# Shift and scale in four parts of 256 features, the first six W_in blocks summed over two K chunks at a time, upper chunks of x transposed behind the lower

## The chip, the cores and the metric

The kernel runs on one core of a Trainium2 chip. Its time is the device time of one execution in microseconds (us). Before the change three runs took 943.0, 944.63 and 945.49 us, median 944.63. The profiled execution took 942.63 us; the span from its first to its last instruction is 940.9 us.

The engines are named as in the profile: PE is TensorE (matrix products and transposes; PEld its weight loads), DVE VectorE, ACT ScalarE, POOL GpSimd, SP SyncE, which issues nearly all loads of weights. Each runs its own instructions in order and waits on semaphores that others raise.

## The reference

One encoder layer is applied to two requests of 256 tokens with 1024 features. Cut to what the change touches:

```
mod = (silu(c) @ w_mod + b_mod).reshape(B, 6, 1, D)        # c: (B, 1024), w_mod: (1024, 6144)
shift1, scale1, gate1 = mod[:, 0], mod[:, 1], mod[:, 2]    # and shift2, scale2, gate2
h = LN(x) * (1 + scale1) + shift1                          # (256, 1024) for each request
z = h @ w_in + b_in                                        # w_in: (1024, 5120): u, v, p, gates
a = gelu(u) * (W_s @ LN(gelu(v)) + b_s)                    # v is the segment computed first
...                                                        # pooling branch, merge, W_out, LN
out = mixture of experts: top group of 4, top 2 of its 8 experts, 32 experts of 3 x 2 MB
```

All is float32. Large products split each operand in a high part (rounded to the type fp32r) and the remainder as a low part, and sum three products: high x high, low x high, high x low.

## The kernel before

Tokens of both requests lie side by side (512 columns), features on the partitions in 8 chunks of 128 (`KC = 8`). The stages in order are: load x, its mean and variance (DVE), normalise (DVE), transpose on PE to chunks of features, copy out of PSUM (ACT) into `n_t`; shift and scale of the features; then 56 blocks of 128 output features (`NBLK`), 5.5 us of PE each in the steady state; then the output projection, routing and 32 experts.

The change lies in the first 60 us. Shift and scale come from `w_mod[:, 0:2048]` (8 MB). Before the change this is done in two parts of 512 features each, because h of chunk 0 needs the sum over all 1024 rows of `w_mod` but only its own columns:

- `first_mod_unit(part, q)` multiplies two row chunks of `w_mod` by silu(c) into the PSUM bank `MOD`. The four products of one round (shift and scale, two row chunks) go to four groups of 32 columns of the array. Four units make a part. DVE adds the bias (`first_mod_rows`), PE transposes the row into columns in bank `COL` (`first_mod_columns`), DVE sums and adds 1 (`first_scales`).
- With the scales of a part, ACT writes the high half of h, `h_hi` (`h_high`), DVE and POOL the full h in `h32`, and DVE the low half `h_lo` (`h_low`).
- The first six blocks of W_in (`FIRST = 6`) are summed in the same two parts of 4 chunks, in six PSUM banks kept open. ACT writes the high part of a piece of W_in (`part_split_hi`), DVE the low part (`first_split_lo`, `split_lo`). Blocks 0 and 1 go as a pair, chunk by chunk as h arrives (`part_pair`), the others in turn (`part_block`). After the second part's pair, ACT evaluates gelu on finished blocks and PE transposes them back (`transposes`).
- `keep_clock` is a product whose result nobody reads.

SP issues the loads in one queue and in this order: x, part 0 of `w_mod` (8 loads of 512 KB), part 0 of W_in, part 1 of both, then `load_mod(8)` and on: the 16 loads of 1 MB with the other 4096 columns of `w_mod`, into two buffers in turn (`modraw`), used by `mod_unit_at` between blocks, and among them `load_unit(2)`, the next 2 MB of W_in. `load_mod(m)` waits until `m - 1` units have been multiplied (`pe_mod`), since its buffer must be free. A load of an expert or of W_in later in the kernel is released by the work on PE in the same way. POOL issues 2.3 MB of loads for later stages (`ws_raw`, `wp_raw`, `bs_bc` and small ones) when all of `h_lo` is written (`pool.wait_ge(dve_hlo, KC)`); PE needs `ws_raw` after block 5, just ahead of unit 2 of `mod_unit_at`.

Of the kernel before, what the change touches and what calls it, by code (L numbers as in the profile page):

```python
# [36 lines left out]
PART = KC // 2  # L37
H_DIRECT = (0, 1, 4, 5)
H_VECTOR = (3, 0, 7, 4)
H_POOL = (2, 1, 6, 5)  # L40


def hybrid_encoder(nc, x_prompt, x_sample, c_prompt, c_sample, w_mod, b_mod, w_in, b_in, w_spatial,
# [12 lines left out]
    with ctx:  # L56
# [5 lines left out]
        def sem(name):  # L62
# [20 lines left out]
        modraw0 = [at(f"modraw0_{i}", [128, 2, 2, 512], f32, o)  # L83
                   for i, o in enumerate([2 * SLOT + 8 * K * j for j in range(4)] + [32 * K, 40 * K] + [SLOT + 32 * K, SLOT + 40 * K])]
# [42 lines left out]
        modrow_first = at("modrow_first", [128, 2, 512], f32, S0 + 9728 + 4096)  # L127
# [259 lines left out]
        def first_mod_source(part, kc):  # L387
            return w_mod[0, 128 * kc:128 * kc + 128, 0:2048].rearrange("p (v f n) -> p v f n", v=2, f=2)[:, :, part, :]

        def halves_of_chunks(tiles, turn):  # L390

            first = PART * (turn // 2 % 2)
            return tiles[turn % 2][:, first:first + PART, :]

# [44 lines left out]
        def _(sp):  # L439
            def load_unit(u):  # L440
                if u >= 2:
                    sp.wait_ge(dve_wlo, FIRST + 4 * (u - 1))
# [8 lines left out]
            for part in range(2):  # L451
                for kc in range(KC):
                    m = 4 * part + kc // 2
                    landed = s_m0[4 + kc // 4 if part else kc // 2]
                    sp.dma_start(modraw0[m][:, kc % 2, :, :], first_mod_source(part, kc)).then_inc(landed, 16)
                chunks = slice(PART * part, PART * part + PART)
                if part == 0:
# [3 lines left out]
                    sp.dma_start(raw[:, 1, chunks, :], unit_source(1)[:, chunks, :]).then_inc(s_wpre[2], 16)  # L461
                else:
                    for u in range(2):
                        sp.dma_start(raw[:, u, chunks, :], unit_source(u)[:, chunks, :]).then_inc(s_w[u], 16)
# [93 lines left out]
        def _(pool):  # L558
# [4 lines left out]
            for v in range(2):  # L563
                for r in range(REQ):
                    pool.dma_start(modrow_first[64 * v + r:64 * v + r + 1, :, :],
                                   b_mod[0:1, 1024 * v:1024 * v + 1024].rearrange("a (f n) -> a f n", f=2)).then_inc(s_bmod, 16)
# [4 lines left out]
            for kc in H_POOL:  # L571
# [142 lines left out]
        def _(pe):  # L714
# [15 lines left out]
            def first_mod_unit(part, q):  # L730
# [4 lines left out]
                for k in range(2):  # L735
                    for v in range(2):
                        j = 2 * v + k
                        x = mm(MOD[32 * j:32 * j + 32, :], silu_c[:, 2 * q + k, :], modraw0[4 * part + q][:, k, v, :], start=(q == 0), stop=(q == 3))
                x.then_inc(pe_mod, 1)

            def first_mod_columns(part):
                pe.wait_ge(dve_row0, part + 1)
                for k in range(4):
# [3 lines left out]
            for _ in range(3):  # L747
                keep_clock(512)
            pe.wait_ge(act_pro, 1)

            def n_columns(i):
                pe.wait_ge(dve_n, i + 1)
                if i >= 2:
                    pe.wait_ge(act_nt, 2 * (i - 1))
                for kc in range(KC):
                    bank = B[2 * (i % 2) + kc // 4]
                    x = pe.transpose(bank[:, 128 * (kc % 4):128 * (kc % 4) + 128], xin[:, i, 128 * kc:128 * kc + 128], ident)
                x.then_inc(pe_xt, 1)

            first_mod_unit(0, 0)  # L760
            n_columns(0)
            n_columns(1)
            first_mod_unit(0, 1)
            n_columns(2)
            n_columns(3)
            first_mod_unit(0, 2)
            first_mod_unit(0, 3)
            keep_clock(256)
            pe.wait_ge(act_nt, 2 * TILES)
            pe.wait_ge(dve_pro, 1)  # L770
            first_mod_columns(0)
            keep_clock(512)
# [1771 lines left out]
```

## Time and profile before

| | |
|---|---|
| median of three runs | 944.63 us |
| the profiled execution | 942.63 us, span 940.9 us |
| PE busy | 897.1 us, 95% of the span |
| DVE, ACT, POOL busy | 381.0, 243.1, 118.1 us |
| moved by DMA | 295.3 MB, mean 314 GB/s |
| first product of h with W_in | 27.16 us from the start |
| end of the pair of part 1 | 54.34 us from the start |

The profile's times are microseconds from the span's start. A timeline row is: start, duration, engine, line, operation, output<-input, shapes, number of instructions merged, and in brackets how long the engine was idle before it and who released it. One float32 product or unit product shows as two records of MATMUL (a product of 128x512 in the form fp32r as one). A DMA row gives the number of DMAs, KB each and the median time from issue to landing.

### The profile page before, as it was taken

Reading aid. Unit: us, or ns where it says so; the run is one execution under the profiler, and the core shown is the slowest. Engines: PE = TensorE matmul, PEld = TensorE weight load, DVE = VectorE, ACT = ScalarE, POOL = GpSimd, SP = SyncE. Lnnn points to the kernel's source line nnn. Section 1 sums busy time; section 2 is a strip of 40 time slices with the busy share of each in tenths; the row PEclk is TensorE's granted clock in tenths of the full one; section 3 lists DMA queues with packets and bytes.
Section 4 is the critical chain, followed back from the end, with each engine's and each line's share of the span. In section 5 each row is a group of like instructions: output and inputs, shape, how many; then the busy total and the mean of one; then the engine's idle time right before and its main releaser. Section 6 shows DMA issues by size and latency. Waiting matters only on the chain. (4 is left out here: it accounts for less than half of the span.)

```text
span 940.9 us, 12139 instructions
## 1 busy us (share of the span) xinstructions
PE 897.1 (95%) x4420; PEld 547.3 (58%) x4420; DVE 381.0 (40%) x657; ACT 243.1 (26%) x360; POOL 118.1 (13%) x149
## 2 busy tenths in 40 slices
PE   5999999999999999999999999998998999999894
PEld 2677767888888888787544444444444344444331
DVE  5543434565344236798622322222122132321346
ACT  3342335331333225446410111011011101110113
POOL 3130556000001000000000000000000100000041
PEclk9999999999999999999999999999999999999997
DMA  9975676274665623908999999999999999999993
GB/s 341 363 246 191 224 269 224 90 267 179 222 225 153 183 90 101 300 1 367 399 384 419 427 426 426 426 427 427 429 426 425 424 387 428 429 427 427 422 412 122
DMA packets 51291, 295.32 MB, mean 314 GB/s; under 512 B 5438, under 2 KB 6558, under 8 KB 35986
## 3 DMA queue, kind: packets, MB, share of 16 engines
q1 hardware_dynamic: 40784, 263.47, 69.9%
q0 software_dynamic: 9952, 29.80, 9.4%
q10 hardware_dynamic: 482, 1.13, 0.3%
q8 instruction: 39, 0.64, 0.3%
q14 instruction: 34, 0.28, 0.1%
HBM read 275.81 MB, written 22.83 MB: 317 GB/s over the span
## 5 line engine op out<-in xcount | busy, mean ns | idle before, releaser
L716 PE MATMUL banks<-down_w,hid_t 128*64 128x512 f32 x512 | 119.7, 610 | 11.9 <-issue 10.9
L716 PE MATMUL banks<-h_hi,w_hi 128*128 128x512 f32 x320 | 125.0, 391 | 0.5 <-ACT h_hi L1398 0.5
L716 PE MATMUL banks<-h_lo,w_hi 128*128 128x512 f32 x320 | 125.2, 398 | 0.0
L716 PE MATMUL banks<-h_hi,w_lo 128*128 128x512 f32 x320 | 124.8, 390 | 0.0
L716 PE MATMUL banks<-up_w,x_by_expert 128*64 128x512 f32 x256 | 112.6, 593 | 0.0
L716 PE MATMUL banks<-gate_w,x_by_expert 128*64 128x512 f32 x256 | 112.5, 592 | 0.0
L716 PE MATMUL banks<-up_w,x_by_pair 128*64 128x512 f32 x240 | 105.4, 592 | 0.0
L716 PE MATMUL banks<-gate_w,x_by_pair 128*64 128x512 f32 x240 | 105.4, 592 | 0.0
L1615 ACT ACTIVATE sg_hid<-banks 64x512 f32<-64x512 f32 x33 | 19.5, 592 | 313.8 <-PE banks L716 313.8
L2177 DVE TENSOR_TENSOR sg_hid<-banks,sg_hid 64x512 f32<-64x512 f32 x32 | 22.2, 694 | 177.9 <-ACT sg_hid L1615 177.9
L685 POOL DMA_INDIRECT round_y<-yout,store_row x30 | 31.0, 1034 | 461.5 <-DVE yout L2300 448.7
L1806 DVE TENSOR_TENSOR w_lo<-raw,w_hi 128x1024 fp32r<-128x1024 f32 x50 | 61.4, 1228 | 67.0 <-ACT w_hi L1353 66.9
L716 PEld LDWEIGHTS banks<-down_w,hid_t 128*64 128x64 f32 x512 | 36.3, 140 | 72.2 <-issue 65.2
L716 PEld LDWEIGHTS banks<-gate_w,x_by_expert 128*64 128x64 f32 x256 | 34.9, 137 | 70.8 <-issue 70.7
L1353 ACT ACTIVATE w_hi<-raw 128x1024 fp32r<-128x1024 f32 (+1 forms) x62 | 59.8, 970 | 61.2 <-PE banks L716 54.3
L716 PEld LDWEIGHTS banks<-h_lo,w_hi 128*128 128x128 f32 x320 | 60.1, 188 | 25.1 <-issue 8.4
L716 PEld LDWEIGHTS banks<-gate_w,x_by_pair 128*64 128x64 f32 x240 | 32.9, 137 | 66.5 <-issue 66.5
L716 PE MATMUL banks<-sel_group,h_hi 128*128 128x256 f32 x256 | 69.7, 306 | 0.0
L2300 DVE TENSOR_TENSOR yout<-banks,yout 128x512 f32<-128x512 f32 x32 | 22.1, 691 | 112.9 <-PE banks L716 112.8
L716 PEld LDWEIGHTS banks<-h_hi,w_hi 128*128 128x128 f32 x320 | 60.2, 188 | 12.7 <-ACT h_hi L1398 1.1
L716 PEld LDWEIGHTS banks<-h_hi,w_lo 128*128 128x128 f32 x320 | 60.1, 188 | 12.7
L716 PE MATMUL banks<-sel_group,h_lo 128*128 128x256 f32 x256 | 63.6, 282 | 1.4 <-issue 1.4
(331 smaller groups left out, 1314.7 us busy)
## 6 DMA issues: line engine op xcount, KB each, us to landing
down_w<-in_w_exp_down SPq DMA_DIRECT2D x29, 2048.0 KB, 20.5
gate_w<-in_w_exp_gate SPq DMA_DIRECT2D x28, 2048.0 KB, 18.5
up_w<-in_w_exp_up SPq DMA_DIRECT2D x28, 2048.0 KB, 22.9
modraw<-in_w_mod SPq DMA_DIRECT2D x16, 1024.0 KB, 4.9
raw<-in_w_in SPq DMA_DIRECT2D x8, 2048.0 KB, 9.7
round_y<-zrow POOLq DMA_DIRECT2D x6, 2048.0 KB, 7.6
modraw<-in_w_mod SPq DMA_DIRECT2D x16, 512.0 KB, 11.4
down_w<-in_w_exp_down SPq DMA_DIRECT2D x6, 1024.0 KB, 14.8
```

The costliest lines, as they stand in the source:

```text
L685: pool.indirect_dma_start(round_halves, bass.IndirectOffsetOnAxis(store_row[:, e:e + 1], 0), yout[s][:, :], None, bounds_check=2 * LAST_RO ...
L716: return pe.matmul(out, lhsT, rhs, start=start, stop=stop, skip_group_check=True)
L1353: return act.activation(out, in_, ACT.Copy, scale=scale)
L1615: act.activation(sgb[0:CAP, :], bank[0:CAP, :], ACT.Silu).then_inc(sm["silu"], 1)
L1806: dve.tensor_tensor(w_lo[par][:, :, :], raw[:, u % 2, :, 128 * (b % 4):128 * (b % 4) + 128], w_hi[par][:, :, :].bitcast(f32), ALU.subtract ...
L2177: dve.tensor_tensor(sg_hid[CAP:128, :], B[0][CAP:128, :], sg_hid[0:CAP, :], ALU.mult).then_inc(m_sem["hid"], 1)
L2300: dve.tensor_tensor(yout[s][:, :], B[1][:, :], yout[s][:, :], ALU.mult).then_inc(m_sem["yo"], 1)
```

## The change

The constant `NPART = 4` takes the place of two parts: a part is now 2 chunks of 128 features (`PART = 2`), with 256 columns each of shift and scale (`WIDE = 256`). It does the following.

- The 8 MB of `w_mod` come in 32 loads of 256 KB, and W_in in pieces of 2 chunks. PE waits for 4 loads, then for 8, in part 0, and for all 8 of a part after that. The units of a part (products 256 wide) stand together behind block 2 of the part before.
- The transposes of x are cut in lower chunks (0 to 3) and upper chunks (4 to 7). The lower ones come first; the upper ones of tiles 1 to 3 follow the column transposes of part 0. On ACT, `n_copied` of the upper chunks stands behind `h_high(0)` and block 2's split.
- All eight chunks of `h_hi` are written by ACT directly from `n_t`; even chunks of `h32` come from DVE, odd ones from POOL.
- Of three `keep_clock(512)` ahead of the first unit one is left, and the two behind the column transposes are gone.
- `load_mod(8)` waits for 8 units instead of 7 (`max(KC, m - 1)`); `pe_mod` now counts two units at a time, two per part, so that it reaches 8 in part 3's units.
- The first six blocks are multiplied in four parts, in banks kept open over all four.

```
-PART = KC // 2
-H_DIRECT = (0, 1, 4, 5)
-H_VECTOR = (3, 0, 7, 4)
-H_POOL = (2, 1, 6, 5)
+NPART = 4
+PART = KC // NPART
+WIDE = 128 * PART
+BEFORE = FIRST * (NPART - 1)
...
             def load_mod(m):
-                sp.wait_ge(pe_mod, m - 1)
+                sp.wait_ge(pe_mod, max(KC, m - 1))
...
-            for part in range(2):
+            for part in range(NPART):
                 for kc in range(KC):
-                    m = 4 * part + kc // 2
-                    landed = s_m0[4 + kc // 4 if part else kc // 2]
-                    sp.dma_start(modraw0[m][:, kc % 2, :, :], first_mod_source(part, kc)).then_inc(landed, 16)
+                    landed = s_m0[part + 1 if part else kc // 4]
+                    sp.dma_start(modraw0[part][kc // 2][:, kc % 2, :, :], first_mod_source(part, kc)).then_inc(landed, 16)
...
-            for kc in H_POOL:
+            for kc in range(1, KC, 2):
                 pool.wait_ge(dve_col, 2 * (kc // PART) + 2)
...
+            def first_mod_units(part, first, last):
                 if part == 0:
-                    pe.wait_ge(s_m0[q], 32)
+                    pe.wait_ge(s_m0[first // 2], 64)
                 else:
-                    pe.wait_ge(s_m0[4 + q // 2], 64)
...
+                    pe.wait_ge(s_m0[part + 1], 128)
+                for q in range(first, last):
+                    for k in range(2):
+                        for v in range(2):
+                            j = 2 * v + k
+                            x = mm(MOD[32 * j:32 * j + 32, 0:WIDE], silu_c[:, 2 * q + k, :], modraw0[part][q][:, k, v, :], start=(q == 0), stop=(q == 3))
+                    if q % 2 == 1:
+                        x.then_inc(pe_mod, 1)
...
-            for _ in range(3):
-                keep_clock(512)
+            keep_clock(512)
             pe.wait_ge(act_pro, 1)
...
-            part_pair(0)
-            first_mod_unit(1, 0)
-            part_block(0, 2)
-            first_mod_unit(1, 1)
-            part_block(0, 3)
-            first_mod_unit(1, 2)
-            first_mod_unit(1, 3)
-            part_block(0, 4)
-            pe.wait_ge(dve_col, 1)
-            first_mod_columns(1)
-            part_block(0, 5)
-            part_pair(1)
+            for part in range(NPART - 1):
+                part_pair(part)
+                part_block(part, 2)
+                first_mod_units(part + 1, 0, 4)
+                part_block(part, 3)
+                first_mod_columns(part + 1)
+                part_block(part, 4)
+                part_block(part, 5)
+            part_pair(NPART - 1)
...
             for i in range(TILES):
-                act.wait_ge(pe_xt, i + 1)
-                for hb in range(2):
-                    copy(n_t[:, 4 * hb:4 * hb + 4, 128 * i:128 * i + 128],
-                         B[2 * (i % 2) + hb][:, :].rearrange("p (k n) -> p k n", k=4)).then_inc(act_nt, 1)
...
+                n_copied(i, 0)
             part_split_hi(0, 0)
             part_split_hi(0, 1)
+            act.wait_ge(act_nt, TILES)
             h_high(0)
-            for b in range(2, FIRST):
-                part_split_hi(0, b)
-            part_split_hi(1, 0)
-            part_split_hi(1, 1)
-            h_high(1)
+            part_split_hi(0, 2)
+            n_copied(0, 1)
+            n_copied(1, 1)
+            part_split_hi(0, 3)
+            n_copied(2, 1)
+            n_copied(3, 1)
+            part_split_hi(0, 4)
+            part_split_hi(0, 5)
+            act.wait_ge(act_nt, 2 * TILES)
+            for part in range(1, NPART):
+                part_split_hi(part, 0)
+                part_split_hi(part, 1)
+                h_high(part)
+                if part < NPART - 1:
+                    for b in range(2, FIRST):
+                        part_split_hi(part, b)
...
+            for part in range(NPART):
+                first_mod_rows(part)
+                part_split_lo(part, 0)
+                if part:
+                    part_split_lo(part, 1)
+                first_scales(part)
+                dve.wait_ge(dve_col, 2 * part + 2)
+                if part == 0:
+                    part_split_lo(part, 1)
+                elif part == 2:
+                    dve.wait_ge(act_nt, 2 * TILES)
+                modulated(PART * part)
+                for kc in range(PART * part, PART * part + PART):
+                    h_low(kc)
+                if part < NPART - 1:
+                    for b in range(2, FIRST):
+                        part_split_lo(part, b)
```

PE, before, from the first product on the constants to the first product of h with W_in (`cst` are constants, `modraw` pieces of `w_mod`, `xin` normalised rows of x, `modrow_first` shift and scale as rows):

```order
L716 MATMUL banks<-cst 128x512 x3
L716 MATMUL banks<-modraw_0_68,silu_c 32x512 x4
L757 MATMUL banks<-cst,xin 128x128 x16
L716 MATMUL banks<-modraw_1_69,silu_c 32x512 x4
L757 MATMUL banks<-cst,xin 128x128 x16
L716 MATMUL banks<-modraw_2_70,silu_c 32x512 x4
L716 MATMUL banks<-modraw_3_71,silu_c 32x512 x4
L716 MATMUL banks<-cst 128x256
L744 MATMUL banks<-cst,modrow_first 128x128 x4
L716 MATMUL banks<-cst 128x512
L716 MATMUL banks<-cst 128x256
L716 MATMUL banks<-h_hi,w_hi_80 128x512
```

PE, after, the same place:

```order
L719 MATMUL banks<-cst 128x512
L719 MATMUL banks<-modraw_0_0_68,silu_c 32x256 x4
L719 MATMUL banks<-modraw_0_1_69,silu_c 32x256 x4
L719 MATMUL banks<-cst 128x256
L766 MATMUL banks<-cst,xin 128x128 x12
L719 MATMUL banks<-modraw_0_2_70,silu_c 32x256 x4
L719 MATMUL banks<-modraw_0_3_71,silu_c 32x256 x4
L766 MATMUL banks<-cst,xin 128x128 x8
L751 MATMUL banks<-cst,modrow_first 128x128 x2
L766 MATMUL banks<-cst,xin 128x128 x12
L719 MATMUL banks<-h_hi,w_hi_88 128x512
```

Twelve of the 32 transposes of x have moved behind the column transposes, and the units are half as wide.

ACT, before, from the copies of the transposed x to the pieces of W_in that follow `h_hi` (`n_t` is x normalised and transposed, `h` the full h):

```order
L1353 ACTIVATE n_t<-banks 128x4x128 x8
L1353 ACTIVATE w_hi_80<-raw 128x512
L1353 ACTIVATE w_hi_81<-raw 128x512
L1398 ACTIVATE h_hi<-n_t,mod_t,scale1p 128x256 x4
L1353 ACTIVATE h_hi<-h_115 128x512 x2
L1353 ACTIVATE w_hi_80<-raw 128x512
L1353 ACTIVATE w_hi_81<-raw 128x512
```

ACT, after, the same place:

```order
L1359 ACTIVATE n_t<-banks 128x4x128 x4
L1359 ACTIVATE w_hi_88<-raw 128x256
L1359 ACTIVATE w_hi_89<-raw 128x256
L1405 ACTIVATE h_hi<-n_t,mod_t,scale1p 128x256 x4
L1359 ACTIVATE w_hi_88<-raw 128x256
L1359 ACTIVATE n_t<-banks 128x4x128 x2
L1359 ACTIVATE w_hi_89<-raw 128x256
L1359 ACTIVATE n_t<-banks 128x4x128 x2
```

Four of the eight copies of x now stand behind `h_hi`, and the first splits are half as wide.

## Rows read from the trace of the kernel before

**Rows 1.** The page, part 1: busy time, share of the span, instructions.

```profile
PE 897.1 (95%) x4420; PEld 547.3 (58%) x4420; DVE 381.0 (40%) x657; ACT 243.1 (26%) x360; POOL 118.1 (13%) x149
```

**Rows 2.** Timeline of PE up to the first product of h with W_in.

```profile
10.37 5.49 PE L716 MATMUL banks<-cst 128*128 128x512 f32 x6
...
18.93 1.06 PE L716 MATMUL banks<-modraw,silu_c 128*32 128x512 f32 x8
19.93 1.97 PE L757 MATMUL banks<-cst,xin 128*128 128x128 f32 x16
21.82 1.92 PE L716 MATMUL banks<-modraw,silu_c 128*32 128x512 f32 x16
...
25.20 1.46 PE L716 MATMUL banks<-cst 128*128 128x512 f32 x4
27.16 0.50 PE L716 MATMUL banks<-h_hi,w_hi 128*128 128x512 f32 x1 [0.51 <-ACT h_hi L1398]
```

**Rows 3.** Timeline of DVE: normalising, first scales, one full split.

```profile
14.05 2.98 DVE L1786 TENSOR_SCALAR xin<-xin,mv,rs 128x1024 f32<-128x1024 f32 x4
...
23.89 0.69 DVE L1816 TENSOR_TENSOR modrow_first<-banks,modrow_first 128x512 f32<-128x512 f32 x1 [6.73 <-PE banks L716]
24.50 0.68 DVE L1811 TENSOR_TENSOR w_lo<-raw,w_hi 128x512 fp32r<-128x512 f32 x1
25.40 0.17 DVE L1822 COPY mod_t<-banks 128x16 f32<-128x16 f32 x1 [0.21 <-PE banks L744]
...
68.79 1.22 DVE L1806 TENSOR_TENSOR w_lo<-raw,w_hi 128x1024 fp32r<-128x1024 f32 x1 [0.54 <-ACT w_hi L1353]
```

**Rows 4.** Timeline of ACT: copies, first splits, first h_hi, one full split.

```profile
21.06 2.06 ACT L1353 ACTIVATE n_t<-banks 128x512 f32<-128x512 f32 x4 [0.83 <-PE banks L757]
22.98 1.17 ACT L1353 ACTIVATE w_hi<-raw 128x512 fp32r<-128x512 f32 x2
26.02 2.08 ACT L1398 ACTIVATE h_hi<-n_t,mod_t,scale1p 128x256 fp32r<-128x256 f32 x4 [1.86 <-DVE scale1p L1825]
...
67.71 1.05 ACT L1353 ACTIVATE w_hi<-raw 128x1024 fp32r<-128x1024 f32 x1
```

**Rows 5.** Loads issued from 1.8 to 3.0 us: KB each, us to landing.

```profile
modraw<-in_w_mod SPq DMA_DIRECT2D x2, 512.0 KB, 10.0
```

**Rows 6.** Windows: PE, PEld, DVE, ACT, POOL busy, granted clock, DMA share, GB/s.

```profile
10.00:15.00 5.00, 4.93 (x7) 2.02 (x7) 4.45 (x14) 1.69 (x3) 0.00 (x0) 1.00 1.06 382
```

**Rows 7.** Timeline of PE: part 1's pair, and what follows it.

```profile
48.73 0.39 PE L716 MATMUL banks<-h_hi,w_hi 128*128 128x512 f32 x1
...
52.36 1.98 PE L716 MATMUL banks<-h_lo,w_hi 128*128 128x512 f32 x8
54.89 0.66 PE L825 MATMUL banks<-cst,g 128*128 128x128 f32 x4 [0.55 <-ACT g L1432]
...
71.54 1.06 PE L716 MATMUL banks<-modraw,silu_c 128*32 128x512 f32 x8
...
78.64 1.06 PE L716 MATMUL banks<-modraw,silu_c 128*32 128x512 f32 x8
```

**Rows 8.** Timeline of SP's queue: load_mod(10), load_unit(2).

```profile
56.60 0.33 SPq L447 DMA_DIRECT2D modraw<-in_w_mod  x1
57.30 0.38 SPq L443 DMA_DIRECT2D raw<-in_w_in  x1
```

**Rows 9.** Loads issued at 56.6 us: load_mod(10), beside POOL's.

```profile
modraw<-in_w_mod SPq DMA_DIRECT2D x1, 1024.0 KB, 11.3
```

**Rows 10.** Loads issued at 57.3 us: load_unit(2).

```profile
raw<-in_w_in SPq DMA_DIRECT2D x1, 2048.0 KB, 16.6
```

**Rows 11.** Loads issued at 64.2 us: load_mod(11).

```profile
modraw<-in_w_mod SPq DMA_DIRECT2D x1, 1024.0 KB, 12.2
```

**Rows 12.** Loads issued from 41 to 43 us: load_mod(8) and (9).

```profile
modraw<-in_w_mod SPq DMA_DIRECT2D x2, 1024.0 KB, 5.6
```

**Rows 13.** Timeline of POOL: the first of its loads.

```profile
51.90 0.99 POOL L579 DMA_DIRECT2D ws_raw<-in_w_spatial  x1 [2.64 <-DVE h_lo L1840]
```

More of the change, by code:

```diff
@@ L741, in first_mod_columns @@
             def first_mod_columns(part):
                 pe.wait_ge(dve_row0, part + 1)
-                for k in range(4):
+                if part:
+                    pe.wait_ge(dve_col, 2 * part - 1)
+                for k in range(PART):
                     x = pe.transpose(COL[:, 128 * k:128 * k + 128], modrow_first[:, part, 128 * k:128 * k + 128], ident)
                 x.then_inc(pe_modcol, 1)
-            for _ in range(3):
-                keep_clock(512)
+            keep_clock(512)
@@ L749, in _ @@
             pe.wait_ge(act_pro, 1)
[L751 to L757, printed above, removed]
-                x.then_inc(pe_xt, 1)
-            first_mod_unit(0, 0)
-            n_columns(0)
@@ L762, in _, with n_columns @@
[L762 to L767, printed above, removed]
-            keep_clock(256)
-            pe.wait_ge(act_nt, 2 * TILES)
+            def n_columns(i, hb):
+                bank = B[i if hb == 0 else (4, 5, 0, 1)[i]]
+                if hb == 0:
+                    pe.wait_ge(dve_n, i + 1)
+                elif i >= 2:
+                    pe.wait_ge(act_nt, i - 1)
+                for k in range(4):
+                    first = 512 * hb + 128 * k
+                    x = pe.transpose(bank[:, 128 * k:128 * k + 128], xin[:, i, first:first + 128], ident)
+                x.then_inc(pe_xt, 1)
@@ L770, in _ @@
+            first_mod_units(0, 0, 2)
+            keep_clock(256)
+            n_columns(0, 0)
+            n_columns(0, 1)
+            n_columns(1, 0)
+            first_mod_units(0, 2, 4)
+            n_columns(2, 0)
+            n_columns(3, 0)
             pe.wait_ge(dve_pro, 1)
             first_mod_columns(0)
-            keep_clock(512)
-            keep_clock(256)
+            for i in range(1, TILES):
+                n_columns(i, 1)
             def block_at(b, i, mov_hi, mov_lo, freed, count):
-                pe.wait_ge(act_whi, FIRST + b + 1)
-                pe.wait_ge(dve_wlo, FIRST + b + 1)
+                pe.wait_ge(act_whi, BEFORE + b + 1)
+                pe.wait_ge(dve_wlo, BEFORE + b + 1)
@@ new lines, in n_copied, with h_high @@
+            def n_copied(i, hb):
+                act.wait_ge(pe_xt, ((1, 3, 4, 5), (2, 6, 7, 8))[hb][i])
+                copy(n_t[:, 4 * hb:4 * hb + 4, 128 * i:128 * i + 128],
+                     B[i if hb == 0 else (4, 5, 0, 1)[i]][:, :].rearrange("p (k n) -> p k n", k=4)).then_inc(act_nt, 1)
+            def h_high(part):
+                act.wait_ge(dve_col, 2 * part + 2)
+                for kc in range(PART * part, PART * part + PART):
+                    for r in range(REQ):
+                        x = act.activation(h_hi[:, kc, SEQ * r:SEQ * r + SEQ], n_t[:, kc, SEQ * r:SEQ * r + SEQ], ACT.Identity,
+                                           scale=scale1p[:, kc, r:r + 1], bias=mod_t[:, 0, kc, r:r + 1])
+                    x.then_inc(act_hhi, 1)
```

124 lines of the change are left out of this document (45 added, 79 removed).

## The prediction

> **What bounds the kernel now.** I read the page's busy times first: PE works 95% of the span [rows 1], so a microsecond counts only where PE stands still or is given more or less work. Next came PE's timeline up to the first product of h with W_in [rows 2]: that product starts at 27.16 us, released by ACT. Behind it PE has work without a break until the pair of part 1 ends at 52.36 + 1.98 = 54.34 us [rows 7]. What comes later than 27.16 only because the start is late moves up with it, unless a load is missing. So two questions decide: how much earlier the start is, and whether the loads issued between 41 and 65 us, which wait for PE, can follow.
>
> The chain to the start, from the timelines of DVE and ACT: the last unit ends at 21.82 + 1.92 = 23.74; DVE adds the bias at 23.89 and ends the first scales at 26.0 [rows 3]; ACT writes h_hi 0 at 26.02 in two instructions of 0.52 [rows 4]; PE starts at 27.16.
>
> **The start, step by step.** Rows of x are normalised from 14.05, one every 0.745 (2.98 / 4) [rows 3]; this doesn't change. The first two loads of `w_mod`, 512 KB each, issued at 1.9 and about 2.4, take 10.0 us [rows 5], so the first megabyte is there at about 12.8; the new first four loads are the same bytes. The second megabyte follows at 382 GB/s [rows 6], 1.05 MB / 382 GB/s = 2.7 us later: 15.6. Before, two further megabytes were needed.
>
> PE: the first products on constants run at half the pace: 5.49 / 3 = 1.83 us for 128x512 [rows 2], against 1.46 us for one of 512 and one of 256 at 25.20, or 0.97 for 512. That is the 1.2 GHz level against 2.4, though the granted clock already reads 1.00 there [rows 6]; I go by the pace. One such product: to 12.2. PE waits until 12.9. A unit 512 wide at full pace costs 1.92 - 1.06 = 0.86 us [rows 2]; at half width and half pace the same: two, with 0.3 at the ends, to 14.9; the product of 256 on constants to 15.8. Before, full pace was there at 17 us, after 6 us of work; I take it here from 15.8. Twelve transposes at 1.97 / 16 = 0.12 [rows 2]: 17.3. Two units of 0.43 and 0.15: 18.3. Eight transposes: 19.3. ACT then copies the last lower chunk, 0.52 [rows 4]: 19.9; splits block 0, 256 wide. A split of 512 costs 1.17 / 2 = 0.58, one of 1024 1.05 [rows 4]; 256 is not in the trace. Its bounds are 0.2 (half of 512, no fixed part) and 0.58; the line through the two rows gives 0.35 to 0.4, which I take: 20.3. DVE's low part (0.68 at 512, 1.22 at 1024 [rows 3], so 0.42): 20.75. The scales follow it in DVE's order, 25.40 to 26.02 = 0.62: 21.4. Two instructions of ACT and the hand-over, 1.14 as before: **first product at 22.6, 4.5 us earlier.** Both queues of waits matter here: behind DVE's split, which waits for ACT, stand the scales that ACT waits for.
>
> **What moves behind the start.** Before, four units ran after the first product: two alone at 1.06 - 0.06 and two together at 1.86, 3.9 us. Now twelve of half width do: 12 x 0.43 + 3 x 0.15 = 5.6. Half width might not halve the time; bounds 0.25 and 0.86 a unit, 3.5 and 10.8 in all; since the four column groups work side by side and each round is 0.43 long at 512, I stay near half. Column transposes: three times two for once four, 0.75 for 0.36 (0.66 with its tail for four [rows 7]). Gaps between groups: +0.2. Together 2.3 us. The 144 products of the six blocks are the same number in both kernels, as is their pace, (52.36 - 48.73) / 16 = 0.227 [rows 7]. The lead when block 5 ends is thus **4.5 - 2.3 = 2.2 us**.
>
> The other edits cost nothing on the path. ACT now writes all eight h_hi with 2 x 0.52 each where two of four had 0.57, about 2 us more ACT work; a part holds 36 x 0.227 + 1.9 + 0.4 + 0.5 = 10.9 us of PE work and 6.5 of ACT's. If that cover were gone, 0.5 us per part would show. The upper copies stand behind h_hi 0 and 1; block 2 needs the first at about 25.4, and it is done near 24.4. The twelve late transposes, 1.5 us, fit between 19.6 and 22.6, where PE waits anyway. The 8 loads of part 1 are wanted at 22.6 + 4.1 = 26.7 and land near 24 (another 0.8 + 2.1 MB behind 15.6 at 382 GB/s is 23.2). After that a part's 3.1 MB comes every 8.3 us, and PE takes 10.9 us for a part, so the slack grows.
>
> **What the lead meets.** The end of the pair of the last part: 22.6 + 120 x 0.227 + 5.6 + 0.75 + 1.4 (the gaps that the same stretch has now, 27.18 - 96 x 0.227 - 3.9 - 0.36 = 1.1, for 120 products) = 57.6, **3.3 us later** than 54.34, though only half a part is left after it. And that point, not block 5, releases the loads: load_mod(10) waits for the unit behind the pair (issued 56.60 now [rows 8], then about 59.7), load_unit(2) for the split of block 3 behind the pair (57.30 now [rows 8], then about 60), POOL's 2.3 MB for the last h_low (51.90 now [rows 13], then about 55.5). The loads of 8 and 9 are issued at 50.3 instead of about 42 and take 5.6 [rows 12]: in time.
>
> load_mod(10) lands 11.3 us after its issue, being moved beside POOL's loads [rows 9]: at 67.9 now, at 71.0 then. PE uses it at 71.54 now [rows 7]; with blocks 2 to 5 at 1.37 us instead of 2.74 it wants it at 57.6 + 17.2 - 5.5 = 69.3 and **waits 1.7**. Then one unit, block 6 and transposes (71.54 to 78.64, 7.1 us [rows 7]): 78.1. Unit 3 needs load_mod(11), which stands behind load_unit(2) in SP's queue: that one lands at 57.30 + 16.6 = 73.9 [rows 10] and load_mod(11) at 64.2 + 12.2 = 76.4 [rows 11], so the queue, not its issue, sets it. The queue starts 3.1 us later with the same bytes: 79.5. Bounds: 76.4 if the queue makes up everything, 80.2 if POOL's shift of 3.6 counts in full. I take 79.5, from the shift of the SP loads. Now unit 3 starts at 78.64. **Sum: 79.5 - 78.64 = +0.9 us**; behind it PE has its loads in time (load_mod(12) is issued behind unit 2 and used a whole block later than 11), and the difference stays to the end.
>
> 942.63 + 0.9 = 943.5 in terms of the profiled execution. This one lies 2.0 under the median of the runs, so I predict 944.63 + 0.9 = **945.5 us**.
>
> **The rivals.** *The lead survives.* The loads come in time since load_mod(10) and POOL's loads overlap less than now. For it: 10 and 11 have 3.6 and 2.2 us in hand now. Against: both are issued by the event that moves later. Gives -2.2: 942.4. Chance 0.20.
>
> *The start is earlier still.* If the low splits and scales follow sooner (PE at full pace from the beginning, 1.2 us less; splits at 0.2, 0.4 less), the start is near 21, the pair ends at 56, the loads cost nothing: -3.8, 940.8. Against: nothing shows full pace before 16 us. Chance 0.12.
>
> *PE stays at half pace.* The two removed products leave it idle from 12.2 to 12.9 and feed it narrow units. If full pace comes one stretch of work later, near 19, the 12 transposes cost 1.5 more and the two units 0.9: start 24.9, pair end 59.9, the queue 5.4 later, load_mod(11) at 81.8: +3.1, **947.7**, slower. It decides from about 1 us of half pace behind 15.8. For it: the busy stretch before full pace was unbroken. Chance 0.15.
>
> *Small loads.* If a load of 256 KB takes the 1.36 us of 512 KB, the eight of part 0 land where they do now, the start stays at 27.2, the pair ends at 62.2, load_mod(11) at 84.1: +5.5, 950.1. For it, nothing in the rows but that no load of this size is there; 512 KB at a time the queue gives 382 GB/s [rows 6]. Chance 0.05.
>
> On this last case the Trainium skill (DMA: Bandwidth & Descriptors, section Rules for kernel authors) says that one should have at least 1 MiB per DMA for the most bandwidth. The trace's 382 GB/s with half of that doesn't bear it out for loads that queue one behind the other, which is why the chance is small.
>
> **How the numbers follow.** Forecast 0.48; its own range 943.8 to 947. A measurement tells this kernel from no change at about 0.3%, 2.8 us. Faster by more (under 941.8): 0.10 of the second rival, 0.08 of the first, 0.02 of the forecast: 0.20. Slower by more (over 947.4): 0.09, 0.05, and 0.05 of the forecast: 0.19. The same: 0.61. The range 941.2 to 948.8 leaves out the small loads and the ends of the others.
>
> **What would show it.** First product of h with W_in at 22.6 (21.5 to 25). Units of four at 1.9 us a part. End of the last part's pair at 57.6. PE idle ahead of unit 2, released by the load, 1 to 3 us; again ahead of unit 3, up to 1.5. Unit 3's start against 78.64 is the whole effect: if it is under 77, the lead survived and the step on the queue is wrong; if the first product is later than 24, the clock or the loads' size is it. A change of span that differs from unit 3's shift would put the cause behind 80 us, where I claim none.

## The result, and the profile after

The changed kernel took 951.12 us, median of five runs (945.48 to 953.11), against 944.63 (943.0 to 945.49; by now five runs too) before: ratio 1.0063, 95% interval 1.0045 to 1.0082. Forecast were 945.5, a range of 941.2 to 948.8, and a chance of 0.19 for slower. Nine more runs in a second set gave 948.62 (945.97 to 952.21) against 944.17, ratio 1.0046 [1.0027, 1.0065]. So by the ratios the change costs 4 to 6 us where +0.9 was forecast. The profiled execution (945.48 us, span 943.8) is the fastest of its five, so its trace holds the smallest part of the loss. Below, unit n is the n-th unit of `mod_unit_at`, counted from 0, which multiplies what load_mod(8 + n) brings.

The page, part 1, answers to [rows 1]: PE has less work than before and a longer span.

```profile
span 943.8 us, 12332 instructions
PE 895.0 (95%) x4476; PEld 548.7 (58%) x4476; DVE 382.8 (41%) x677; ACT 246.6 (26%) x376; POOL 118.5 (13%) x149
```

PE's timeline up to the first product of h with W_in, after (columns as in [rows 2]):

```profile
10.46 2.07 PE L719 MATMUL banks<-cst 128*128 128x512 f32 x2
14.08 1.93 PE L719 MATMUL banks<-modraw,silu_c 128*32 128x256 f32 x16 [1.55 <-DMA modraw<-in_w_mod]
15.95 1.22 PE L719 MATMUL banks<-cst 128*128 128x256 f32 x2
16.96 2.77 PE L766 MATMUL banks<-cst,xin 128*128 128x128 f32 x12
19.66 1.40 PE L719 MATMUL banks<-modraw,silu_c 128*32 128x256 f32 x16
20.99 1.09 PE L766 MATMUL banks<-cst,xin 128*128 128x128 f32 x8
21.92 0.38 PE L751 MATMUL banks<-cst,modrow_first 128*128 128x128 f32 x2
22.14 1.47 PE L766 MATMUL banks<-cst,xin 128*128 128x128 f32 x12
25.25 0.50 PE L719 MATMUL banks<-h_hi,w_hi 128*128 128x512 f32 x1 [1.63 <-ACT h_hi L1405]
```

The first megabyte is there at 14.1, not 12.9, in a stretch that now moves 344 GB/s instead of 382 [rows 6] (its first loads of 256 KB take 8.7 us, those of 512 KB took 10.0 [rows 5]). Not only the loads are smaller: from 10 to 20 us 3775 of 3790 packets are under 2 KB, where before 459 of 2277 were. The first twelve transposes take 2.77 us, while the last twelve take 1.47: half pace lasts until about 20 us, not 15.8. The product that was forecast for 22.6 comes at 25.25.

```profile
10.00:15.00 5.00, 3.28 (x15) 1.22 (x19) 4.45 (x14) 1.69 (x3) 0.00 (x0) 1.00 1.11 344
```

ACT's and DVE's rows for the narrow splits, after, answer to [rows 3, 4]: two splits of 256 take 0.72 on ACT, one low part 0.42 on DVE, as estimated.

```profile
22.66 0.72 ACT L1359 ACTIVATE w_hi<-raw 128x256 fp32r<-128x256 f32 x2
```

```profile
23.11 0.42 DVE L1826 TENSOR_TENSOR w_lo<-raw,w_hi 128x256 fp32r<-128x256 f32 x1 [1.47 <-ACT w_hi L1359]
```

PE's timeline from the last part's units on, after; it answers to [rows 7]:

```profile
50.67 1.93 PE L719 MATMUL banks<-modraw,silu_c 128*32 128x256 f32 x32
...
58.81 1.07 PE L719 MATMUL banks<-h_lo,w_hi 128*128 128x512 f32 x4
...
71.42 1.09 PE L861 MATMUL banks<-cst,ws_raw 128*128 128x128 f32 x8 [0.65 <-DMA bs_bc<-in_b_spatial]
72.95 1.07 PE L719 MATMUL banks<-modraw,silu_c 128*32 128x512 f32 x8 [0.44 <-DMA modraw<-in_w_mod]
...
83.23 1.07 PE L719 MATMUL banks<-modraw,silu_c 128*32 128x512 f32 x8 [3.10 <-DMA modraw<-in_w_mod]
```

Before, PE waits at none of these places, and unit 3 starts at 78.64; now it waits 0.65 + 0.44 + 3.10 us and starts unit 3 at 83.23, 4.6 later. The first of the three waits is for POOL's `bs_bc`, which the prediction didn't name. This shift goes on to the experts' first load, which PE's work releases. SP's queue there, before and then after:

```profile
380.43 0.34 SPq L478 DMA_DIRECT2D gate_w<-in_w_exp_gate  x1
```

```profile
385.02 0.34 SPq L481 DMA_DIRECT2D gate_w<-in_w_exp_gate  x1
```

The queues, after, answer to [rows 8 to 13]. POOL's first load comes at 58.22, 6.3 us later than before:

```profile
58.22 1.00 POOL L582 DMA_DIRECT2D ws_raw<-in_w_spatial  x1 [1.84 <-DVE h_lo L1852]
```

load_mod(8) and (9) are issued at 52.7 and take 5.9 us, load_mod(10), issued at 62.1, takes 10.8, and load_unit(2) and load_mod(11), issued at 62.52 and 66.99, the following (DMA rows of one issue each). 66.99 + 16.2 = 83.2 is the start of unit 3.

```profile
raw<-in_w_in SPq DMA_DIRECT2D x1, 2048.0 KB, 18.2
```

```profile
modraw<-in_w_mod SPq DMA_DIRECT2D x1, 1024.0 KB, 16.2
```

The span itself grew by 2.9 us only (940.9 to 943.8), 1.7 less than unit 3's shift. The prediction would read such a difference as a cause behind 80 us. But the stretch from the experts' first load to the end takes 558.8 to 563.6 us in the fourteen traces of this document (560.5 before), and the longest belongs to **small_before**, which has the code of the kernel before there. What moves it was not looked into; a single trace's total doesn't measure this change, so below, traces are compared at the experts' first load, and totals by the ratios.

### The profile page after: what moved, and what is told of

It is laid out like the page before. It is cut to its first block and busy times, and to the rows that moved or that the text cites. A ratio compares the mean times of both kernels' runs of the same rounds, so it can differ in the third digit from the quotient of the medians.

```text
span 943.8 us, 12332 instructions
## 1 busy us (share of the span) xinstructions
PE 895.0 (95%) x4476; PEld 548.7 (58%) x4476; DVE 382.8 (41%) x677; ACT 246.6 (26%) x376; POOL 118.5 (13%) x149
## 5 line engine op out<-in xcount | busy, mean ns | idle before, releaser
L2186 DVE TENSOR_TENSOR sg_hid<-banks,sg_hid 64x512 f32<-64x512 f32 x32 | 22.2, 695 | 184.3 <-ACT sg_hid L1630 182.9
L719 PEld LDWEIGHTS banks<-gate_w,x_by_pair 128*64 128x64 f32 x240 | 32.9, 137 | 67.3 <-issue 67.3
## 6 DMA issues: line engine op xcount, KB each, us to landing
down_w<-in_w_exp_down SPq DMA_DIRECT2D x6, 1024.0 KB, 10.8
```

The lines of the kernel that those rows point to most:

```text
L719: return pe.matmul(out, lhsT, rhs, start=start, stop=stop, skip_group_check=True)
L2186: dve.tensor_tensor(sg_hid[CAP:128, :], B[0][CAP:128, :], sg_hid[0:CAP, :], ALU.mult).then_inc(m_sem["hid"], 1)
```

## The experiments

Twelve kernels ran in three groups, each group with runs of the kernel before on the same chip (medians 944.17, 944.3 and 943.04). "Landing" is the landing of load_mod(11), counted from POOL's first load; where PE waits for it, it is the start of unit 3, and elsewhere the issue plus the time to landing. "Waits" are those of PE for loads from block 5 to unit 3. All times are us of one profiled execution, except the ratio.

| kernel | first product | POOL's first load | landing | waits | unit 3 | experts' first load | ratio to before, interval |
|---|---|---|---|---|---|---|---|
| before | 27.16 | 51.90 | 24.5 | 0 | 78.64 | 380.43 | 1 |
| changed | 25.25 | 58.22 | 25.0 | 4.2 | 83.23 | 385.02 | 1.0063 [1.0045, 1.0082] |
| again | 23.35 | 56.27 | 26.2 | 5.3 | 82.45 | 385.63 | 1.0046 [1.0027, 1.0065] |
| clock | 22.13 | 55.07 | 25.9 | 5.1 | 80.96 | 384.32 | 1.0035 [1.0020, 1.0050] |
| later | 24.63 | 57.54 | 26.4 | 0 | 84.90 (a block later) | 380.45 | 0.9981 [0.9966, 0.9996] |
| both | 22.00 | 54.97 | 26.2 | 0 | 82.36 (a block later) | 377.90 | 0.9976 [0.9961, 0.9991] |
| early | 23.64 | 56.58 | 26.1 | 5.3 | 82.71 | 387.37 | 1.0048 [1.0032, 1.0064] |
| all | 22.90 | 55.87 | 25.7 | 0 | 83.27 (a block later) | 378.88 | 0.9967 [0.9955, 0.9979] |
| pool | 24.51 | 57.48 | 22.6 | 1.7 | 80.07 | 381.86 | 1.0007 [0.9991, 1.0024] |
| fill | 23.73 | 56.69 | 25.7 | 2.1 | 85.46 | 388.21 | 1.0068 [1.0042, 1.0094] |
| small_before | 26.68 | 51.56 | 21.5 | 0 | 78.32 | 380.11 | 0.9998 [0.9987, 1.0009] |
| best | 23.30 | 56.22 | 22.6 | 0 | 83.61 (a block later) | 379.19 | 0.9974 [0.9956, 0.9992] |
| pool_clock | 23.46 | 56.46 | 22.2 | 1.4 | 78.64 | 380.46 | 0.9967 [0.9951, 0.9982] |
| fill2 | 24.71 | 57.66 | 26.0 | 2.6 | 84.22 | 386.00 | 1.0033 [1.0020, 1.0046] |

**again**, the changed kernel as it is.

> The changed kernel as it is, timed again beside the other three of this call, with a second trace. Why: its profiled execution took 945.48 us, but its median was 951.1, and the mean granted clock of its five runs went from 0.992 (945.5 us) down to 0.982 (952.6 us). Theory A (the loads): the loss up to 90 us is the same in every run, +4 to +5 us at unit 3 of mod_unit_at, and what is over it comes later, from the clock. Theory B (the early clock): in the slow runs full pace comes later still in the first 30 us, or falls again behind the 3.1 us for which PE waits ahead of unit 3. A expects unit 3 near 83 us in this trace too, B expects it at 85 or later if this trace is of a slow run. Median expected 948 to 952.

The start was nearly on forecast this time (first product 23.35, last pair's end 56.85 + 1.07 = 57.9, unit 2 at 71.3), and yet load_mod(11) landed at 82.45, three us behind its forecast. The start accounts for 0.75 of them; the rest is the queue itself. PE's rows, then windows (columns as in [rows 6]):

```profile
82.45 1.94 PE L719 MATMUL banks<-modraw,silu_c 128*32 128x512 f32 x8 [3.99 <-DMA modraw<-in_w_mod]
84.31 0.80 PE L719 MATMUL banks<-h_lo,w_hi 128*128 128x512 f32 x1
```

```profile
68.00:70.00 2.00, 1.09 (x8) 0.76 (x7) 1.74 (x2) 1.81 (x3) 0.00 (x0) 1.00 1.03 243
70.00:72.00 2.00, 1.57 (x16) 0.74 (x14) 1.31 (x2) 0.05 (x1) 0.00 (x0) 1.00 1.06 197
...
80.00:82.00 2.00, 0.00 (x0) 0.00 (x0) 0.96 (x1) 1.01 (x1) 0.00 (x0) 1.00 0.60 254
82.00:84.00 2.00, 1.55 (x8) 0.20 (x8) 0.27 (x1) 0.00 (x0) 0.00 (x0) 0.52 0.31 131
84.00:86.00 2.00, 2.00 (x9) 1.42 (x6) 0.00 (x0) 0.00 (x0) 0.00 (x0) 0.62 0.40 61
```

Two things were not in the prediction: from 68 to 72 us the queues are full (share 1.03 and 1.06) but move only 243 and 197 GB/s, and behind PE's idle time the granted clock falls to 0.52, the lower level. Unit 3 at +3.8 becomes the experts' load at +5.2. So both theories have a part: unit 3 is near 83 us as in A, and what is over it follows the wait, as in B, without a later start.

**clock**, one more product ahead of the first unit.

```
-            keep_clock(512)
+            for _ in range(2):
+                keep_clock(512)
```

> One more product on constants (128x512) ahead of the first units, where PE stood idle from 12.5 to 14.1 us. If that gap is what kept PE at half pace until about 20 us, full pace comes near 16 us, the first product of h with W_in moves from 25.3 to 23.0-23.8, unit 3 from 83.2 to about 81.5, and the kernel gains about 1.5 us on the changed one. If the gap is not it (the narrow products are), the start stays at 25 and nothing changes.

Full pace came with the first units (16 records in 1.07 us), and the first product at 22.13, against the 22.6 forecast for the change itself. But PE still waited 1.03 + 0.74 + 3.29 us, and the clock fell behind that. A start 1.2 us earlier than in **again** brought 1.3 at the experts' load; the ratio is 0.0011 lower, with intervals that overlap.

**later**: unit 2 and the transposes of ws_raw behind block 6, unit 3 behind block 7, unit 4 with unit 5.

```
-                if n == 5:
+                if n == 6:
...
-                if n in (1, 3, 5, 6, 7):
-                    mod_unit_at({1: 0, 3: 1, 5: 2}.get(n, n - 3))
+                if n in (1, 3, 6, 7):
+                    mod_unit_at({1: 0, 3: 1, 6: 2, 7: 3}[n])
...
+                if n == 0:
+                    mod_unit_at(4)
```

> Units 2 and 3 of mod_unit_at and the transposes of ws_raw one block later each (unit 2 behind block 6, unit 3 behind block 7, unit 4 beside unit 5 behind block 8); the same work on PE. Theory A (PE waits for loads that the end of the pair releases): the three waits, 0.65 + 0.44 + 3.1 = 4.2 us, go, and the end of block 6 and all behind it moves up by about 4 us; unit 5 at its place within 0.5 us of the kernel before; time 4 us under the changed kernel. Rival (PE would have lost it anyway, at the next load): the waits come back at units 3 to 5 and the gain is under 1 us.

No load is waited for, and the whole loss is gone, though the start was at half pace until about 20 us in this trace. The loss is these waits and what follows from them. load_mod(11) still lands 26.4 us behind POOL's first load, at 83.9; unit 3 now wants it at 84.90. PE's rows of units 2 and 3, then SP's of the experts' first load (380.43 before):

```profile
77.80 1.06 PE L719 MATMUL banks<-modraw,silu_c 128*32 128x512 f32 x8
...
84.90 1.06 PE L719 MATMUL banks<-modraw,silu_c 128*32 128x512 f32 x8
```

```profile
380.45 0.34 SPq L481 DMA_DIRECT2D gate_w<-in_w_exp_gate  x1
```

**both**: the last two edits together.

> Both edits, the product on constants and the later units. If each works by itself and they add, first product near 23.4, no waits, and the experts' first load is issued at 380.4 + 0.4 - 1.7 = about 379 us (380.43 before, 385.02 in the changed kernel): 1 us faster than the kernel before, within what can be told. If only the loads count, as later.

In the traces the gains add up: the start is 2.6 us earlier than in **later** and the experts' load as much, 2.5 before that of the kernel before. In the ratio 0.9976 beside 0.9981 doesn't show it, with intervals that overlap. No load is waited for; 0.77 us without a releaser stand ahead of block 6, as in **later**.

**early**: load_mod(8) and (9) issued at 38.4 us instead of 52.7, into buffers that are free by then.

```
-            [32 * K + 4 * K * j for j in range(4)], [SLOT + 32 * K + 4 * K * j for j in range(4)]))]
+            [32 * K + 4 * K * j for j in range(4)], [16 * K + 4 * K * j for j in range(4)]))]
...
-                sp.wait_ge(pe_mod, max(KC, m - 1))
+                if m >= 10:
+                    sp.wait_ge(pe_mod, m - 1)
```

> The changed kernel, with load_mod(8) and load_mod(9) (2 MB) issued right behind the first W_in pieces instead of at 52.7 us: the third part's first buffers lie in space that is free until ws_raw is written. Queue theory: in the changed kernel these 2 MB are on the queues when POOL's loads and load_mod(10) are issued, and they push the landing of load_mod(11) back; 2 MB at some 400 GB/s are 5 us, of which about 2 overlap. Without them load_mod(11) lands 1.3 to 2.4 us sooner, PE's wait ahead of unit 3 falls from 3.1 to between 1 and 2 us, the experts' first load is issued 1.3 to 2.4 us earlier (383.0 to 384.3), and the median falls by 1.5 to 2, to about 0.9970 of the changed kernel's ratio, so 1.0025 against before. Rival, the load stream from POOL's issue to load_mod(11) sets the landing by itself: no change, ratio 1.0046.

The rival holds: nothing was moved from 52 to 58 us, and load_mod(11) still landed 26.1 us behind POOL's first load. The 2 MB of load_mod(8) and (9) were not what pushed it back. The clock fell behind the wait for longer than in the runs so far (windows, granted clock third from the end):

```profile
82.00:84.00 2.00, 1.29 (x8) 0.20 (x8) 0.55 (x1) 0.00 (x0) 0.00 (x0) 0.51 0.35 147
84.00:86.00 2.00, 2.00 (x7) 1.16 (x4) 0.00 (x0) 0.00 (x0) 0.00 (x0) 0.50 0.29 53
86.00:88.00 2.00, 2.00 (x6) 1.58 (x5) 0.00 (x0) 0.00 (x0) 0.00 (x0) 0.50 0.84 315
```

Unit 3 starts 4.1 us later than before, the experts' load 6.9: 2.9 are added behind the fall.

**all**: both and early.

> The kernel with two products of 512 columns to hold the clock at the start and with units 2, 3 and 4 one block later (it measured 0.9976 against before), and with load_mod(8) and load_mod(9) issued right behind the first W_in pieces. Queue theory: PE no longer waits for a load there, so an earlier landing is worth nothing: ratio 0.9976 within 0.001, the experts' first load at 377.9. Rival, the loads still cost there in a way that the waits don't name (the 0.77 us without a releaser at block 6): 0.5 to 1 us faster.

PE waits for no load in either kernel, and the experts' load came 1.0 us later than in **both**, with the start 0.9 later. The ratio, 0.9967 beside 0.9976 with intervals that overlap, fits the theory and the rival alike.

**pool**: four small loads behind POOL's windows instead of ahead of them.

```
-            pool.dma_start(wr[:, :, 0:NGRP], w_router_group[0, :, :].rearrange("(p k) n -> p k n", p=128)).then_inc(s_wr, 16)
-            pool.dma_start(wr[:, :, NGRP:], w_router_expert[0, :, :].rearrange("(p k) n -> p k n", p=128)).then_inc(s_wr, 16)
-            pool.dma_start(br_bc[:, 0:NGRP], b_router_group[0, :].partition_broadcast(128)).then_inc(s_wr, 16)
-            pool.dma_start(br_bc[:, NGRP:], b_router_expert[0, :].partition_broadcast(128)).then_inc(s_wr, 16)
...
             pool.wait_ge(dve_d, 8)
+            (the same four)
             pool.dma_start(sgu_bc[:, 0, :], sgu_g[0, :].partition_broadcast(128)).then_inc(s_sgu, 16)
```

> The changed kernel, with POOL's four small router loads (the router's weights and biases) issued behind its pooling windows instead of ahead of them. Theory one, the queue is long because of these loads of many small pieces: bs_bc and load_mod(11) land 1 to 2 us sooner, the experts' first load comes as much earlier, the median falls by 1 to 2. Theory two, the queue is long because of its bytes, of which these loads are few: load_mod(11) within 0.5 us of where it was behind POOL's issue (24.5 to 26.4 us), ratio 1.0046 within 0.0015.

Theory two fell, and theory one forecast too little. These loads are 0.16 MB, and load_mod(11) lands 22.6 us behind POOL's first load instead of 25.0 to 26.4 in the nine traces that have them there. The windows show where; the same stretch as that shown for **again**, without the slow two:

```profile
68.00:70.00 2.00, 2.00 (x12) 1.49 (x10) 1.22 (x2) 1.81 (x3) 0.00 (x0) 1.00 0.97 391
70.00:72.00 2.00, 1.12 (x9) 0.86 (x8) 2.00 (x3) 1.26 (x2) 0.00 (x0) 1.00 1.03 389
```

The queue that POOL's loads go through tells the same, from 57 to 90 us, in the changed kernel and then in this one (packets, MB, share of 16 engines' time):

```profile
q0 software_dynamic: 736, 2.26, 27.4%
```

```profile
q0 software_dynamic: 592, 2.10, 21.9%
```

0.16 MB less frees (27.4 - 21.9)% x 33 us = 1.8 us of all 16 DMA engines, where at the 391 GB/s of the window the bytes are worth 0.4. The rest of the 2.4 us or more by which the landing moves is not accounted for. PE waits 1.7 us instead of 4.2 to 5.3, and by the two ratios the kernel is 3.7 us faster than in **again**.

**fill**: five products on constants ahead of unit 3's wait.

```
+                if n == 6:
+                    pe.wait_ge(dve_col, 8)
+                    for _ in range(5):
+                        mm(COL[:, :], ident, cst[:, 0:512])
```

> The changed kernel, with five products of 512 columns on constants ahead of unit 3's wait for its load. They add no path, since PE waits there for 3 to 4 us. Theory, a wait of PE of 4 us there makes the granted clock fall behind it (unit 3 at 1.94 instead of 1.07 us a group): with the wait cut by some 1.1 us the clock stays at 1.00 behind it, unit 3's eight groups take 1.07, and against a run with the fall the experts' first load is issued up to 0.6 us earlier; in the median 0 to 0.5 us, which three rounds can hardly tell. Rival, the fall has another source: the groups of unit 3 are at 1.9 again in the profile, at a clock of 0.5 to 0.6 from 82 to 86 us.

The pricing was wrong: it took 1.1 us for the five products, and they took 4.46, from 81.07 on. load_mod(11) landed at 82.4, so without them PE would have waited some 1.3 us, and unit 3 started 3.1 us behind the landing. (A further wait of 1.15 us for a load, at 148 us, is in this trace too.) The clock stayed at 1.00 behind them, which tells nothing, since no wait was left. It had fallen earlier in this trace, to 0.64 and 0.51 from 72 to 76 us, behind waits of 0.88 and 1.22 us for bs_bc and load_mod(10).

**small_before**: the kernel before, with the edit of **pool**.

> The kernel before the change, with POOL's four small router loads behind its pooling windows. In its trace the load rate is 253 to 300 GB/s from 64 to 68 us, and PE waits for none of these loads. Theory, the small loads lengthen the queue by 2 to 3 us in any kernel but cost only one that has no slack there: ratio 1.000 within 0.0012, PE without a wait ahead of units 2 and 3 (at 71.5 and 78.6), and 380 GB/s or more in the two-microsecond windows between 64 and 68. Rival, they cost time of their own (in POOL or DVE, or a wait that the rows don't name): faster by 0.1% or more.

The landing comes 3.0 us sooner (24.5 to 21.5) and the time is the same. The windows of 64 to 68 us, before and then with the edit, repeat what **pool** showed, at an earlier time: the small loads lengthen the queue here too, and PE waits for nothing behind them.

```profile
64.00:66.00 2.00, 2.00 (x12) 1.61 (x9) 0.67 (x1) 0.00 (x0) 0.00 (x0) 1.00 1.02 253
66.00:68.00 2.00, 2.00 (x12) 1.69 (x11) 0.44 (x1) 0.88 (x2) 0.00 (x0) 1.00 0.96 300
```

```profile
64.00:66.00 2.00, 2.00 (x10) 1.62 (x10) 0.35 (x1) 0.00 (x0) 0.00 (x0) 1.00 1.02 398
66.00:68.00 2.00, 2.00 (x13) 1.65 (x12) 0.69 (x1) 1.20 (x2) 0.00 (x0) 1.00 1.05 391
```

**best**: all, with the edit of **pool**.

> Two products to hold the clock at the start, units 2, 3 and 4 one block later, load_mod(8) and load_mod(9) early (together 0.9967 against before), and the four small router loads behind the pooling windows. PE waits for no load there any more, so by the queue theory the last edit is worth nothing: ratio 0.9967 within 0.0012, the experts' first load at 378 to 379 us. Rival, the router loads cost elsewhere: 0.5 to 1 us faster.

No further gain: 0.9974, the experts' load at 379.19, 0.3 us behind that of **all** and 0.2 outside the forecast, with a start 0.4 later.

**pool_clock**: clock, with the edit of **pool**.

> The changed kernel with two products of 512 columns at the start instead of one, and with the router loads behind the windows. The sum from the parts: first product near 22.1, end of the last pair near 56.7, POOL's first load at 55.1, load_mod(11) 22.6 us later (as in the run with the router loads moved) at 77.7, unit 3 at 78.0 to 78.7 after waits of 0.5 to 2 us in all, the experts' first load at 379.5 to 380.5, which is 0 to 1 us before the kernel before: ratio 0.9985 to 1.0000. Rival, what the clock gives is lost again in the queue, as in the run with the two products alone, where 1.3 us of start gave 0.9 to 1.3: ratio 1.0005 or more.

Unit 3 starts at 78.64, to the hundredth where it does before (that it is the hundredth is chance), and the experts' load at 380.46. In the ratio it is better than that and than forecast, 0.9967; its profiled run is the slowest of its seven, so the trace's start (23.46, full pace later than in **clock**) may not be typical. Four versions, both, all, best and pool_clock, lie at 0.9967 to 0.9976 with intervals that overlap: all are faster than before by 2.3 to 3.1 us, and the runs rank them neither against each other nor against **later**.

**fill2**: fill with two products instead of five.

> The changed kernel with two products of 512 columns on constants ahead of unit 3's wait; by the run with five (4.46 us) they take 1.8 us, of a wait of 3 to 4. Theory, waits of 3 to 4 us make the clock fall behind them in some runs and not in others, and that is the spread: unit 3 at 1.06 in the profile, no clock under 0.9 from 82 to 90 us, the median 0.5 to 1.5 us below the changed kernel's and its runs closer together, ratio 1.0030 to 1.0040. Rival, the fall does not follow from the wait, or the spread is from the experts: ratio 1.0046 or more, spread as before.

The two took 1.88 us and ended 0.6 us behind the landing of load_mod(11); unit 3 took 1.06, and no window from 82 to 90 us is under 1.00. The clock fell in another place instead, behind a wait of 2.58 us for bs_bc, which landed 15.1 us behind POOL's first load (13.2 to 13.9 in **changed**, **again**, **clock**, **early** and **fill**):

```profile
74.00:76.00 2.00, 2.00 (x9) 0.50 (x2) 0.00 (x0) 0.00 (x0) 0.00 (x0) 0.53 0.92 313
76.00:78.00 2.00, 2.00 (x7) 1.59 (x6) 0.00 (x0) 0.00 (x0) 0.00 (x0) 0.62 1.06 422
```

The ratio is 0.0013 below that of **again**, with intervals that overlap, and the experts' load, at 386.00, is not earlier than in the two traces of the changed kernel. So a gain is not shown.

## Why the prediction was wrong

**Right.** The first product of h comes earlier. What moves behind the start: the units of a part take 1.93 us (forecast 1.9), and from the first product to the end of the last pair there are 34.6 us in both traces of the changed kernel (59.88 - 25.25, 57.92 - 23.35; forecast 57.6 - 22.6 = 35.0). The lead is eaten because the release of the loads stands behind the last part. POOL's loads start 32.9 to 33.0 us behind the first product (forecast 32.9). PE waits ahead of unit 2 (1.1 and 1.3 us, forecast 1.7) and of unit 3, and where the clock doesn't fall behind it, the shift of unit 3 is what arrives at the experts (4.59 and 4.59 in the first trace, 1.43 and 1.43 in **pool**). That **pool** measures 1.0007, +0.7 us, close to the forecast +0.9, is luck: its start was 1.9 us later than forecast and its queue 1.4 shorter.

**The step that failed: "the queue starts 3.1 us later with the same bytes: 79.5".** The prediction took the queue as a fixed length and moved it by the shift of SP's loads, 0.5 below POOL's. By its own numbers load_mod(11) was to land 79.5 - 55.5 = 24.0 us behind POOL's first load; it was 26.2 in **again** and 25.0 in the first trace. With the start's error this closes both: 79.5 + 0.8 + 2.2 = 82.5 and 79.5 + 2.7 + 1.0 = 83.2. So the forecast +0.9 at unit 3 became +3.8 and +4.6; in the first trace the start's error is the larger part of it, in the second the queue's. The upper bound of 80.2 (76.4 + 3.6 is 80.0) was too low for the same reason: both ends assumed that the queue's length is a constant at most as long as now. **pool** and **small_before** show that about 3 us of this length are the four router loads, in both kernels; they were there before too and so don't explain what changed. What makes the queue 0.5 to 1.9 us longer than before (25.0 to 26.4 against 24.5; without the router loads 22.2 to 22.6 against 21.5) is open: load_mod(8) and (9) are excluded by **early**; that load_mod(11) is now issued 8.8 us behind POOL's first load instead of 12.3 goes with it, and was not tried alone.

**The start was priced at its best.** The rival of half pace had 0.15, and its mark, a first product near 24.9, is what four of seven traces come within 0.4 us of: the seven with one product ahead of the first unit have the first h product at 23.35 to 25.25, mean 24.3; the five with two have 22.0 to 23.5, mean 22.8. The prediction took full pace "from 15.8" and gave no reason: that is after 4.7 us of work with a gap in it. It also read the old trace a little late: full pace is there at about 16.3, not 17 (the unit at 15.78 takes 1.32 us, the later ones 1.06), after 5.9 us without a gap. The second product and the closed gap were what reached it; their shares were not separated. The rival priced load_mod(11) at 81.8 and the kernel at 947.7, near the 948.62 of the second set of runs. That is in part luck: **again** started at 23.35, not 24.9, and its queue and its clock made up for it. The 951.12 of the first set lies nearest to the case of small loads, 950.1, whose first product at 27.2 no trace shows.

Of that case a part is seen: with 256 KB the first stretch moves 344 GB/s instead of 382, and PE waits 0.9 to 1.55 us for the first four loads. Smaller packets came with it, and the two were not tried apart. So 382 GB/s at 512 KB was no proof that size doesn't matter in a queue: in the changed kernel's trace, two loads of 1 MB move 426 from 56 to 58 us.

**Missing altogether: the clock behind a wait.** Three of four traces with a wait of 3.1 to 4.0 us ahead of unit 3 have a granted clock of 0.50 to 0.63 behind it (**again**, **clock**, **early**; not the first), and 1.4, 1.6 and 2.9 us are added between unit 3 and the experts' load. In these three traces the granted clock reads 1.00 in every window from 92 to 392 us, and PE's idle time there is that of the kernel before within 0.2 us. The first profile had 4.6 at the experts and no fall. A shift of 3.8 to 4.6 at unit 3 and 0 to 1.4 behind it give 4.6 and 5.2 us at the experts in the two traces of the changed kernel, of the size of the 4 to 6 of the ratios; the runs of that kernel above 948.4 us have no trace. No experiment ties the spread of the runs to the clock: the changed kernel's nine of the second set lie between 946.0 and 952.2, the kernel before's 32 between 942.3 and 948.1.

**The ranking of rivals.** "The lead survives" was the first rival with 0.20, argued from 2.2 and 3.6 us in hand in the old trace. That slack was real, but smaller than the shift of POOL, 4.4 and 6.3 us in the two traces.

## What to carry to other kernels

Slack ahead of a load is measured against the event that releases it, and a change that brings the front earlier can move that event later. Look at such a queue's rate, not only its bytes: here windows with full DMA share and little over half the GB/s marked a few small loads, which cost nothing until PE waited behind them. A wait that PE did not have before is to be priced with a chance of a slow clock behind it (here three of four waits of 3.1 to 4.0 us).

## What the runs showed of the hardware

- Four loads with 0.16 MB (2 to 128 KB each; with them 84 more packets under 512 B in the stretch from 57 to 90 us) come with 4 us in which all queues together move 197 to 243 GB/s (**again**) or 253 to 300 (the kernel before), where it is 389 to 391 and 391 to 398 without them (**pool**, **small_before**). A load behind them lands 3.0 us sooner without them in the kernel before, 2.4 to 4.2 in the changed one. Whether it is their small packets or that they spread rows over partitions was not tried apart.
- A product of 128x512 on float32 constants takes 0.9 us at full pace (five in 4.46, **fill**), four times what a product in fp32r adds (0.227).
- Behind idle times of PE of 2.6 to 4.0 us the granted clock read 0.50 to 0.63 for 4 to 6 us in four traces (**again**, **clock**, **early**, **fill2**), and 0.64 and 0.51 for 4 us behind 0.88 and 1.22 us close together in a fifth (**fill**); behind 3.10 us in the first trace, and behind 1.17 us in **pool_clock**, it stayed at 1.00.
- At the start the pace was half while the granted clock already read 1.00, until 14 to 16.5 us with two products of 512 and no gap behind them (five traces), and until 17 to 20 us with one product and a gap of 0.9 to 1.55 us (seven).
- Loads of 256 KB one behind the other, in packets under 2 KB, moved 344 and 349 GB/s (10 to 15 and 15 to 20 us), loads of 512 KB with four fifths of their packets larger 382 and 385.
